# Fewer key columns in the scores of the first token block (sliding and latent heads)

## What is computed

```python
# sliding: query block n sees key block n-1 and n; for the first block the one before is masked away
logits = jnp.einsum('bnqkgd,bnskd->bnkgqs', qb, kb) * d ** -0.5
rel = BLOCK + jnp.arange(BLOCK)[:, None] - jnp.arange(2 * BLOCK)[None, :]
valid = (rel >= 0) & (rel < WINDOW) & (key_pos >= 0)
# latent: content part and rotary part are added, and the mask is causal
s = (jnp.einsum('bqhd,bshd->bhqs', qn_blk, k_nope)
     + jnp.einsum('bqhr,bsr->bhqs', qr_blk, k_rope)) * scale
s = jnp.where(key_pos[None, :] <= q_pos[:, None], s, -jnp.inf)
```

## Time and profile before

| | |
|---|---|
| median of three runs | 974.35 us (974.05 to 974.49) |
| the profiled execution, its own time | 974.11 us |
| span of its instructions | 972.3 us (1.8 us lie outside) |
| granted clock of PE, mean | 0.984 |
| PE busy | 928.1 us, 95% |
| DVE busy | 718.4 us, 74% |
| ACT busy | 554.0 us, 57% |

### The profile page before, as it was taken

One profiled execution on the slowest core, in us unless ns is written; L12 is line 12 of the kernel. 1 busy time (PEld: TensorE's weight loads), 2 busy tenths in 40 slices (PEclk: granted clock), 3 DMA queues, 4 the chain that ended last, 5 costly groups with the idle time before them and its releaser, 6 DMA issues. The chain is left out here.

```text
span 972.3 us, 17856 instructions
## 1 busy us (share of the span) xinstructions
PE 928.1 (95%) x6188; PEld 840.5 (86%) x6188; DVE 718.4 (74%) x1423; ACT 554.0 (57%) x1107; POOL 55.3 (6%) x53
## 2 busy tenths in 40 slices
PE   6999999999999999879999999999689999999997
PEld 5999998888899999868888888889687888888886
DVE  4999667888765565587688887666898868888652
ACT  4793655665544455666466555445486646655442
POOL 1046300000000010000000000001000000000000
PEclk9999999999999999789999999999899999999999
DMA  9443436666666466203567665674220557666661
GB/s 236 116 131 109 138 102 177 190 201 192 184 169 188 132 194 177 75 1 87 164 184 209 194 187 174 183 187 155 87 88 2 151 162 204 182 191 192 182 184 43
DMA packets 275315, 148.49 MB, mean 153 GB/s; under 512 B 5961, under 2 KB 273210, under 8 KB 275258
## 3 DMA queue, kind: packets, MB, share of 16 engines
q1 hardware_dynamic: 274330, 146.02, 51.9%
q0 software_dynamic: 608, 1.52, 0.6%
q10 hardware_dynamic: 320, 0.20, 0.1%
HBM read 146.39 MB, written 1.06 MB: 152 GB/s over the span
## 5 line engine op out<-in xcount | busy, mean ns | idle before, releaser
L492 PE MATMUL bank<-x,whi 128*128 128x512 f32 x1184 | 408.6, 397 | 4.3 <-DVE wlo L1673 3.3
L491 PE MATMUL bank<-x,wlo 128*128 128x256 f32 x1036 | 289.6, 280 | 0.0
L1541 DVE TENSOR_TENSOR wlo<-raw,whi 128x1024 fp32r<-128x1024 f32 (+3 forms) x184 | 203.2, 1121 | 71.8 <-ACT whi L1120 71.8
L492 PEld LDWEIGHTS bank<-x,whi 128*128 128x128 f32 x1184 | 213.1, 188 | 47.1 <-DVE wlo L1673 4.2
L1120 ACT CAST whi<-raw 128x1024 fp32r<-128x1024 f32 (+3 forms) x184 | 175.1, 963 | 57.5 <-PE bank L477 34.8
L491 PEld LDWEIGHTS bank<-x,wlo 128*128 128x128 f32 x1036 | 195.4, 189 | 6.4
L1673 DVE TENSOR_TENSOR wlo<-raw,whi 128x1024 fp32r<-128x1024 f32 x108 | 131.7, 1220 | 20.6 <-ACT whi L1202 20.6
L475 PE MATMUL bank<-x,whi 128*128 128x256 f32 (+1 forms) x428 | 125.8, 294 | 11.3 <-DVE un L2134 6.1
L476 PE MATMUL bank<-x,whi 128*128 128x256 f32 (+1 forms) x428 | 123.3, 288 | 0.0
L477 PE MATMUL bank<-x,wlo 128*128 128x256 f32 (+1 forms) x428 | 123.2, 288 | 0.0
L492 PE MATMUL bank<-ar,whi 128*128 128x512 f32 x352 | 123.2, 398 | 0.0
(11 more groups left out here) (223 smaller groups left out, 1445.9 us busy)
## 6 DMA issues: line engine op xcount, KB each, us to landing
raw<-in_ffn_w_gate SPq DMA_DIRECT2D x44, 512.0 KB, 4.6
raw<-in_ffn_w_up SPq DMA_DIRECT2D x44, 512.0 KB, 4.3
raw<-in_ffn_w_down SPq DMA_DIRECT2D x32, 448.0 KB, 4.3
raw<-in_w_gate SPq DMA_DIRECT2D x22, 512.0 KB, 4.5
raw<-in_w_up SPq DMA_DIRECT2D x22, 512.0 KB, 3.9
raw<-in_w_in SPq DMA_DIRECT2D x20, 512.0 KB, 3.9
raw<-in_even_w_in SPq DMA_DIRECT2D x18, 512.0 KB, 4.4
raw<-in_ffn_w_down SPq DMA_DIRECT2D x16, 512.0 KB, 4.6
```

Of the source, the lines that this page charges most:

```text
L491: pe.matmul(o[:, 0:T], w[1], x[:, 0], start=False, stop=False, skip_group_check=True)
L492: ins = pe.matmul(o[:, 0:2 * T], w[0], x, start=first, stop=last, skip_group_check=True)
L1541: ins = v.tensor_tensor(l_, x, h_.bitcast(F32), ALU.subtract)
```

## The change

For the first query block (`b` = 0) only the first 128 keys are given as the moving operand, and only the first 128 columns of the block's half of the bank are written; for `b` = 1 nothing changes, since `P * (b + 1)` is then 256. The number of matmuls, their order, the waits and the semaphores stay as they are. DVE reads the same columns as before.

```diff
                 for b in range(NB):
                     for m in range(len(parts[0])):
                         qs = [[x[:, P * b:P * (b + 1)] for x in part[m][0]] for part in parts]
-                        both = mm3_pair([z[:, T * b:T * (b + 1)] for z in zs], qs, [part[m][1] for part in parts],
+                        keys = [[x[:, 0:P * (b + 1)] for x in part[m][1]] for part in parts]
+                        both = mm3_pair([z[:, T * b:T * b + P * (b + 1)] for z in zs], qs, keys,
                                         b == 0 and m == 0, m == len(parts[0]) - 1)
                 for ins in both:
                     ins.then_inc(g("scores_done"), 1)
```

## The result

| | before | after |
|---|---|---|
| median | 974.36 us (14 runs, 973.94 to 979.23) | 978.09 us (14 runs, 975.08 to 982.63) |
| ratio after / before | | 1.0032, 95% interval 1.0017 to 1.0047 |
| profiled execution, its time | 974.11 us | 981.45 us |
| span | 972.3 us | 979.7 us |
| PE's mean granted clock | 0.984 | 0.970 |

The change makes the kernel slower, by 0.3% (3.7 us between the medians), and it spreads the runs: before, 13 of 14 lie within 2 us; after, they lie over 7.5 us. The profiled execution of the changed kernel is one of its slow ones, 3.4 us above its median: what follows explains that execution, whose loss is 7.3 us, and not the 3.7 us between the medians. The forecast was 974.0 us and no difference that can be told.

What follows compares the result with a forecast made beforehand. PE bounds most stages, the latent heads through a chain with DVE close behind. Gains of 0.25 us (latent) and 0.03 us (sliding) gave 973.8 us from the profiled execution, 974.1 from the median; forecast 974.0 us, range 972.8 to 975.2 us.

Steps and rivals of the forecast that it cites:

- The step of a narrow pair: Score matmuls of line 482: two side-by-side matmuls with 128 moving columns take 0.112 us per step, against 0.119 before.
- the upper and lower bounds: Limits on a narrow pair's step: 0.119 us (no gain at all) above, 0.053 us (the columns alone) below.
- The latent ring: Latent heads' repeating chain through PE, ACT and DVE: 4.18 to about 4.14 us; six calls gain 0.25 us.
- the cheaper load: Rival: a pair's two 64-row loads cost less than one full load; 972.3 us or so, chance 0.06.
- the clock's fall among the latent heads: Rival: less streaming lets PE's clock fall in the latent heads; 976.6 us, or 978 with half the periods; chance 0.04.
- The sliding heads at the lower clock: Sliding call at 425.18, mostly at the lower clock: the load fills 0.21 us per step and nothing is gained.
- the last rival: PE's clock falls among the latent heads, chance 0.04; its closing sentence allowed some tenths of a us in the sliding heads.
- The argument against the rival: Latent stage behind its last score batch: PE busy 3.07 of 3.50, then 2.49 of 3.40 us, yet clock stays 1.00.
- the full-height sequence: Trace's unbroken sequence of twelve matmuls, 128 moving columns and 128 weight columns over all 128 rows: 0.112 us apart.

## Why the prediction was wrong, step by step

- The step of a narrow pair, 0.112 us: right. The batch went from 1.70 to 1.66 us, and the upper and lower bounds were not needed.
- The latent ring, 4.18 to about 4.14 us: right, it is 4.13 us. The two rivals that concern it, the cheaper load and the clock's fall among the latent heads, did not come: the clock of the changed kernel's ring stays at 1.00. The profile of the kernel with the latent heads alone agrees.
- The sliding heads at the lower clock gain nothing: right, 1.65 us before and after.
- The step that failed is one sentence at the end of the last rival: "In the sliding heads the clock falls already, and the ring there hangs on DVE; a fall at another moment moves the end by some tenths of a us." The mechanism of the rival was the right one; it was placed in the wrong stage and had a chance of 0.04. The moment of a fall was not what changed, but how long the lower level lasts: 51 us instead of 20 us in the profiled runs. And beyond those 20 us it costs time, because at that level PE is the bound. The stage took 5.25 us more, plus an estimated 2.2 us in the projection behind.
- The two things that would have told were in the rows. In the lower stretch before, PE was busy for 6.36 of 6.80 us, so the ring hangs on DVE at the upper level only; "hangs on DVE" was read from waits summed over both levels. Apart, they say so: PE waited 4.1 us for line 2000 from 411.5 to 425.2 us, at the upper level, and 0.4 us from 425.2 to 432 us, at the lower. And the stage had the clock at both levels within 60 us, while the latent heads kept the upper one throughout: the stage that already changes its level is the one in which taking streaming away could be expected to keep it down for longer. The argument against the rival, that PE kept its clock with no score call at all, was drawn from the latent stage and was true there.
- The size and the range: one profile and three runs within 0.44 us gave the picture of a fixed pattern. It varies from run to run (973 to 979 us for the kernel before beside the experiments), and a range of 972.8 to 975.2 us had no room for that. Even of the 14 runs of the kernel before in the result one took 979.23 us. Of the changed kernel's 14 runs only the fastest, 975.08 us, lies within that range.

What is open: how much of the loss in the 14 runs is due to the phase (the changed kernel's profile has the clock's first fall 0.7 us later, against its score batch, than that of before), since the phase could be moved but not fixed; how often the clock stays down for long in either kernel, since each has one profile; and why two fillers per call with few columns left the time no higher than two with many, which the account by columns does not explain.

## What to carry to other kernels

A matmul that loads its own 128 columns of weights gains next to nothing from streaming 128 columns instead of 256 (0.007 us of 0.119 at the upper clock, nothing at the lower), so in such a place useless columns are almost free, and here they were worth having. Before taking streaming work off PE in a stage that waits on other engines, look in the granted clock for a stage that is already at both levels, and price it with PE at the lower level: who is the bound then? Where a stage of that kind spreads the runs, matmuls without use in PE's waits are worth a try, wide ones: here they brought the time to its lower end.

## What the runs showed of the hardware

- With fillers of the same number, the same weights and the same 9.3 us of PE's busy time, the stage's clock was 0.93 with 256 columns and 0.68 with 16, and the time 974.3 and 984.4 us; the first fall came 19.4 and 13.3 us after the stage's first score batch. PE's busy share in a profile is thus no sure sign that it keeps its clock.
- Two loads of 64 rows on the two halves of the array, side by side, space narrow pairs as one load of 128 rows does: the batch of 12 pairs shrank by 0.04 to 0.05 us, that is 0.007 to 0.008 us for each of the six narrow ones, as the full-height sequence said.
- The kernel before has the same instructions in every run and still took 973.2 to 979.0 us in 35 runs on one chip, with PE's mean clock between 0.968 (979.04 and 978.49 us) and 0.987 (973.43 us).
